# A float32 encoder trunk on one core: q and k products and an output-gate tile placed ahead of the S5 input matrices, the scan shared by two engines, operands moved to PSUM

## The reference, cut to what matters

```python
proj = xn @ w_in                                   # 1024 -> 2048: u, xm, v, o_pre of 512 each
u, xm, v, o_pre = split(proj)
# S5 group: 32 groups of 16 channels, each with 64 complex states
bu = einsum(u, b_bar)                              # b_bar = ((exp(lam*dt) - 1) / lam) * B
states = associative_scan(a_l*a_e, a_l*x_e + x_l)  # diagonal recurrence over the sequence
y = Re(C . states) + D*u ; g = gelu(y) ; y_a = g * sigmoid(g @ w_glu)
# mLSTM group: 4 heads of 128
xc = silu(causal_dwconv(xm, conv_w, conv_b))       # width 4
q, k = xc @ w_q[h], xc @ w_k[h]
gates = concat(q, k, v) @ w_gates + b_gates
h_t = mlstm_chunkwise(q, k, v, gates)              # stabilised matrix memory
y_b = sigmoid(o_pre) * rmsnorm(h_t)
mix = concat(y_a, y_b) @ w_out
```

## Time and profile before

| | |
|---|---|
| median of 3 runs | 1131.56 us (1131.46 to 1132.12) |
| the profiled execution | 1132.59 us, its span 1130.8 us |
| PE busy | 1094.9 us, 97% |
| PEld | 883.0 us, 78% |
| DVE | 649.8 us, 57% |
| ACT | 465.2 us, 41% |
| POOL | 208.8 us, 18% |
| mean granted clock of PE | 0.99 |

### The profile page before, as it was taken

The page is one execution under the profiler, slowest core; times in us unless marked ns, Lnnn a source line. Parts: engine busy times, 40 slices in busy tenths (PEclk is TensorE's granted clock), DMA queues, the critical chain, the costliest instruction groups (busy, mean ns, idle before and its releaser), DMA issues.

```text
span 1130.8 us, 15508 instructions
## 1 busy us (share of the span) xinstructions
PE 1094.9 (97%) x5542; PEld 883.0 (78%) x5542; DVE 649.8 (57%) x871; ACT 465.2 (41%) x671; POOL 208.8 (18%) x312
## 2 busy tenths in 40 slices
...
GB/s 218 167 97 60 91 1 1 167 94 94 93 101 103 93 93 93 96 109 98 107 107 116 68 56 57 21 129 94 106 98 93 93 94 103 99 93 112 94 93 75
DMA packets 36491, 106.73 MB, mean 94 GB/s; under 512 B 7840, under 2 KB 10144, under 8 KB 36320
## 3 DMA queue, kind: packets, MB, share of 16 engines
...
## 4 chain that ended last, share of the span: by engine, by line
PE 82%; DVE 4%; ACT 3%; issue 2%; POOL 0%; DVEq 0%; ACTq 0%; POOLq 0%
PE bank L1401 25%; PE bank L1403 25%; PE bank L1402 25%; PE bank L1743 1%; PE bank L1424 1%; ACT whi L645 1%; PE bank L1765 1%; PE bank L1563 1%; DVE h L1217 1%; PE bank L1596 0%; ACT sq L651 0%; PE bank L1543 0%; DVE xlo L949 0%; DVE wlo L943 0%; POOL ssum L435 0%
## 5 line engine op out<-in xcount | busy, mean ns | idle before, releaser
L1401 PE MATMUL bank<-xhi,whi 128*128 128x512 f32 x992 | 391.4, 395 | 7.6 <-DVE xlo L949 2.9
L1402 PE MATMUL bank<-xlo,whi 128*128 128x512 f32 x992 | 386.7, 390 | 0.0
L1403 PE MATMUL bank<-xhi,wlo 128*128 128x512 f32 x992 | 386.6, 390 | 0.0
L943 DVE TENSOR_TENSOR wlo<-raw,whi 128x1024 fp32r<-128x1024 f32 x177 | 223.5, 1263 | 269.0 <-ACT whi L645 268.4
L645 ACT ACTIVATE whi<-raw 128x1024 fp32r<-128x1024 f32 x177 | 187.1, 1058 | 378.3 <-PE bank L1403 350.6
L1401 PEld LDWEIGHTS bank<-xhi,whi 128*128 128x128 f32 x992 | 186.6, 188 | 52.1 <-issue 6.1
L1403 PEld LDWEIGHTS bank<-xhi,wlo 128*128 128x128 f32 x992 | 186.5, 188 | 39.4
L1402 PEld LDWEIGHTS bank<-xlo,whi 128*128 128x128 f32 x992 | 186.6, 188 | 38.6 <-issue 1.0
L1401 PE MATMUL bank<-ahi,whi 128*128 128x512 f32 (+1 forms) x374 | 142.5, 381 | 0.0
L1403 PE MATMUL bank<-ahi,wlo 128*128 128x512 f32 (+1 forms) x374 | 141.6, 379 | 0.0
L1402 PE MATMUL bank<-alo,whi 128*128 128x512 f32 (+1 forms) x374 | 140.4, 375 | 0.0
...
## 6 DMA issues: line engine op xcount, KB each, us to landing
...
```

The source lines that it names most:

```text
L943: V.tensor_tensor(wlo[:, t % RING, :], raw[:, t % RAWS, :], whi[:, t % RING, :].bitcast(f32), ALU.subtract).then_inc(lo_done, 1)
L1401: MM(dst, wh, rhi, start=start, stop=False)
L1402: MM(dst, wh, rlo, start=False, stop=False)
L1403: return MM(dst, wl, rhi, start=False, stop=stop)
```

## The change

Seven edits, all in the mixer of layer 0:

1. PE: the eight products of q and k, output-gate tile 13 and the gates stand ahead of the S5 transposes and input products. The gates go to bank 7; group b 3 of the transposes waits until DVE has read them.
2. ACT takes q and k out of PSUM, and then rounds tiles 16 and 17, ahead of its copies of the S5 matrices; before, DVE took q out. The S5 matrices lie where the convolution's results did; q and k have places of their own.
3. DVE: the loop makes the remainders up to tile 12; `split_lo(13)` and the three `g_step`s stand behind the loop, then a wait for the gates, their read, and the remainders of tiles 14, 15, 16. `read_out` 0 to 3 come after output gate 0.
4. The clearing of `cdiag` moves to POOL's start, its two copies to ACT ahead of q.
5. The convolution's accumulator is bank 7; in `g_step` one of the two product buffers is bank 5, and the powers are copied to bank 4.
6. The scan: POOL makes four of the seven last sweeps, DVE three, between its last `head_sum` and `head_gate(3)`; PE's S5 output waits for both.
7. ACT loads the table of GELU right behind `head_factor(3)`, and `head_hi(3)` stands ahead of the first GELU.

```diff
@@ layout @@
-O_IN, O_QK, O_O, O_GLU, O_OUT = 0, 12, 16, 20, 24
-O_UP = [32, 102]
+O_IN, O_O, O_GLU, O_OUT = 0, 12, 16, 20
+O_UP = [28, 98]
-IN_BANK = (0, 1, 2, 3, 4, 5, 6, 0, 1, 2, 3, 0, 1, 2, 3, 0, 1, 2, 3, 0)
+IN_BANK = (0, 1, 2, 3, 4, 5, 6, 0, 1, 2, 3, 0, 1, 2, 3, 0)
+QK_BANK = (1, 2, 3, 0)
-    gtmp = at("gtmp", [P, 2, 2, PAIRS, GCH], base)
+    gtmp = at("gtmp", [P, 2, PAIRS, GCH], base)
-    qT = at("qT", [P, HEADS, SEQ], m1_at)
-    kT = at("kT", [P, HEADS, SEQ], m1_at + 8192)
+    m1re = at("m1re", F2, xc_at)
+    m1im = at("m1im", F2, xc_at + 8192)
...
@@ gpsimd @@
+        G.memset(cdiag[:, :, :, :, :], 0.0)
...
+        G.memset(xs[:, 0, :, 0:1], 0.0).then_inc(carry_done, 1)
         a7, b7 = st1[:, :, 0:SUP - 1], st2[:, :, 0:SUP - 1]
-        for i in range(SUP - 1):
+        for i in range(4):
             axpy(XX[:, :, 1:, i], (qk2[:, :, i:i + 1], aj2[:, :, i:i + 1]),
...
@@ scalar @@
-                A(xcf[:, :], cacc[:, :], ACT.Silu).then_inc(xcf_done, 1)
+                A(xcf[:, :], bank[7][:, :], ACT.Silu).then_inc(xcf_done, 1)
...
+        act.wait_ge(c_negated, 1)
+        act.wait_ge(pads_set, 1)
+        for f in range(2):
+            r = slice(STATE * f, STATE * f + STATE)
+            A(cdiag[r, :, :, f, :], bcp[r, 2:4, :].rearrange("p r (j i) -> p r j i", i=GCH),
+              ACT.Copy).then_inc(cdiag_set, 1)
+        for hd in range(HEADS):
+            act.wait_ge(qk_ready, hd + 1)
+            A(qT[:, hd, :], bank[QK_BANK[hd]][:, :], ACT.Copy).then_inc(q_evac, 1)
+        for hd in range(HEADS):
+            act.wait_ge(qk_ready, HEADS + hd + 1)
+            A(kT[:, hd, :], bank[QK_BANK[hd]][:, :], ACT.Copy).then_inc(k_evac, 1)
+        split_hi(T_QK + RING)
+        split_hi(T_O + RING)
         for b in range(8):
             act.wait_ge(m1_ready, b + 1)
...
-        for hd in range(HEADS):
-            act.wait_ge(qk_ready, HEADS + hd + 1)
-            A(kT[:, hd, :], bank[IN_BANK[O_QK + hd]][:, :], ACT.Copy).then_inc(k_evac, 1)
-        split_hi(T_QK + RING)
-        split_hi(T_O + RING)
...
         head_factor(HEADS - 1)
+        act.preload_act_table_set("gelu_apprx_tanh_and_others")
         s5_output(2)
+        head_hi(HEADS - 1)
         s5_gelu(0)
         s5_output(3)
-        head_hi(HEADS - 1)
         s5_gelu(1)
@@ vector @@
+        t5, u5 = gtmp, bank[5][:, :].rearrange("p (r j i) -> p r j i", r=2, i=GCH)
+        qp = bank[4][:, 0:2 * SUP * PAIRS].rearrange("p (r k j) -> p r k j", r=2, j=PAIRS)
         def g_step(s):
-            steps.up(V.tensor_tensor(gtmp[:, 0], gg[:, :, :, 0:GCH], wide(qq[:, 0, s - 1, :]), ALU.mult))
-            steps.up(V.tensor_tensor(gtmp[:, 1], gg[:, :, :, 0:GCH], wide(qq[:, 1, s - 1, :]), ALU.mult))
+            steps.up(V.tensor_tensor(t5[:, :, :, :], gg[:, :, :, 0:GCH], wide(qp[:, 0, s - 1, :]), ALU.mult))
+            steps.up(V.tensor_tensor(u5, gg[:, :, :, 0:GCH], wide(qp[:, 1, s - 1, :]), ALU.mult))
             settle()
             part = slice(s * GCH, (s + 1) * GCH)
-            steps.up(V.tensor_tensor(gg[:, 0, :, part], gtmp[:, 0, 0], gtmp[:, 1, 1], ALU.subtract))
-            V.tensor_tensor(gg[:, 1, :, part], gtmp[:, 0, 1], gtmp[:, 1, 0], ALU.add).then_inc(g_mid, 1)
+            steps.up(V.tensor_tensor(gg[:, 0, :, part], t5[:, 0], u5[:, 1], ALU.subtract))
+            V.tensor_tensor(gg[:, 1, :, part], t5[:, 1], u5[:, 0], ALU.add).then_inc(g_mid, 1)
...
         for t in range(12):
-            if t:
-                wait_tile_used(dve, max(t, 3))
+            wait_tile_used(dve, max(t, 3))
+            if 0 < t < 9:
                 split_lo(t + RING)
-            else:
-                wait_tile_used(dve, 3)
...
-                steps.up(V.tensor_scalar(cacc[:, :], xpad[:, 3:], col("mlw", 4 * m + 3), col("mlb", m),
-                                         ALU.mult, ALU.add))
+                acc = bank[7][:, :]
+                steps.up(V.tensor_scalar(acc, xpad[:, 3:], col("mlw", 4 * m + 3), col("mlb", m), ALU.mult, ALU.add))
...
-                dve.wait_ge(g0_done, 1)
-                dve.wait_ge(q_done, 1)
-            if 8 <= t < 11:
-                g_step(t - 7)
-
-        steps.up(V.memset(cdiag[:, :, :, :, :], 0.0))
...
+        dve.wait_ge(g0_done, 1)
+        dve.wait_ge(q_done, 1)
+        split_lo(T_QK + 1)
+        dve.wait_ge(out_freed, 7)
+        steps.up(V.tensor_copy(qp, qq[:, :, :, :]))
         settle()
-        for f in range(2):
...
-            V.tensor_copy(cdiag[r, :, :, f, :], bcp[r, 2:4, :].rearrange("p r (j i) -> p r j i", i=GCH)
...
+        for step in range(1, 4):
+            g_step(step)
+        dve.wait_ge(gates_ready, 1)
+        V.tensor_scalar(g8[:, :], bank[7][0:104, :], col("bgate", 0, 104), None, ALU.add).then_inc(gates_copied, 1)
+        split_lo(T_QK + 2)
+        split_lo(T_QK + 3)
+        wait_tile_used(dve, T_QK)
+        split_lo(T_QK + RING)
+        out_gate(0)
         for step in range(3):
             read_out(step)
-        dve.wait_ge(m1_ready, 1)
-        for hd in range(HEADS):
-            dve.wait_ge(qk_ready, hd + 1)
-            dve.wait_ge(s5in_ready, 2) if hd == 0 else None
-            V.tensor_copy(qT[:, hd, :], bank[IN_BANK[O_QK + hd]][:, :]).then_inc(out_freed, 1)
         read_out(3)
-        wait_tile_used(dve, T_QK)
-        split_lo(T_QK + RING)
...
-        out_gate(0)
-        dve.wait_ge(gates_ready, 1)
-        V.tensor_scalar(g8[:, :], bank[4][0:104, :], col("bgate", 0, 104), None, ALU.add).then_inc(gates_copied, 1)
...
+        n = SUP - 1
+        a7, b7 = sv1[:, :, 0:n], sv2[:, :, 0:n]
+        for i in range(4, n):
+            dve.wait_ge(carry_done, 1)
+            re, im = qk2[:, :, i:i + 1], aj2[:, :, i:i + 1]
+            steps.up(V.tensor_tensor(a7, re.to_broadcast([P, 2 * PAIRS, n]), XX[:, :, 0:n, SUP - 1], ALU.mult))
+            steps.up(V.tensor_tensor(b7[:, 0:PAIRS], im[:, 0:PAIRS].to_broadcast([P, PAIRS, n]),
+                                     X[1][:, :, 0:n, SUP - 1], ALU.mult))
+            steps.up(V.tensor_tensor(b7[:, PAIRS:], im[:, PAIRS:].to_broadcast([P, PAIRS, n]),
+                                     X[0][:, :, 0:n, SUP - 1], ALU.mult))
+            settle()
+            steps.up(V.tensor_tensor(a7, a7, b7, ALU.add))
+            settle()
+            V.tensor_tensor(XX[:, :, 1:, i], XX[:, :, 1:, i], a7, ALU.add).then_inc(sweep_done, 1)
+            if i < n - 1:
+                dve.wait_ge(sweep_done, i - 3)
         head_gate(HEADS - 1)
@@ tensor @@
+        pe.wait_ge(lo_done, T_QK + 1)
+        pe.wait_ge(xclo_done, HEADS)
+        for b in range(8):
+            hd = b % 4
+            if b < 4:
+                pe.wait_ge(out_freed, max(k + 1 for k in range(12) if IN_BANK[k] == QK_BANK[hd]))
+            else:
+                pe.wait_ge(q_evac, hd + 1)
+            block3(bank[QK_BANK[hd]][:, :], T_QK % RING, b, xchi[:, hd, :], xclo[:, hd, :], True,
+                   True).then_inc(qk_ready, 1)
+        pe.wait_ge(k_evac, 1)
+        project(T_O, O_O)
+        pe.wait_ge(k_evac, HEADS)
+        pe.wait_ge(rms_done, 1)
+        for k in range(12):
+            q = k % 4
+            ins = MM(bank[7][32 * q:32 * q + 8, :], cols("wg")[:, 8 * k:8 * k + 8],
+                     (qT, kT, vT)[k % 3][:, k // 3, :], start=k < 4, stop=k >= 8)
+        ins.then_inc(gates_ready, 1)
         pe.wait_ge(con_in, 16)
         pe.wait_ge(out_freed, 7)
-        pe.wait_ge(rms_done, 1)
         pe.wait_ge(g_built, CH - 4)
         pe.wait_ge(g_mid, 3)
         for b in range(8):
+            if b == 3:
+                pe.wait_ge(gates_copied, 1)
             if b >= 4:
                 pe.wait_ge(m1_copied, b - 3)
...
         pe.wait_ge(scan_done, 1)
+        pe.wait_ge(sweep_done, SUP - 5)
```

More of the change, by code:

```diff
@@ L189, in build @@
     F4 = [P, 2, PAIRS, P]
-    (ff, gg, m1re, m1im, uc, uperm, xchi, xclo, sigo, xs, ksb) = plan(
-        ("ff", F4, f32), ("gg", F4, f32), ("m1re", F2, f32), ("m1im", F2, f32),
+    (ff, gg, qT, kT, uc, uperm, xchi, xclo, sigo, xs, ksb) = plan(
+        ("ff", F4, f32), ("gg", F4, f32), ("qT", [P, HEADS, SEQ], f32), ("kT", [P, HEADS, SEQ], f32),
         ("uc", [P, GROUPS, NCH], f32), ("uperm", [P, 4, SEQ], f32),
@@ L230, in build @@
     pt_at = tail + 4096 + 2112 + 2 * 2048
+    g8 = at("g8", [104, SEQ], pt_at + 4096 + 2560 + 1024 + 64)
     rtmp = at("rtmp", [P, 2, 2, PAIRS, GCH], tail + 4096 + 2112)
@@ L234, in build @@
     st2 = at("st2", [P, 2 * PAIRS, SUP], pt_at + 1024)
+    sv1 = at("sv1", [P, 2 * PAIRS, SUP], pt_at - 4096)
+    sv2 = at("sv2", [P, 2 * PAIRS, SUP], pt_at - 2048)
     fre, fim = ff[:, 0, :, :], ff[:, 1, :, :]
@@ L291, in build @@
     x_back, cdiag_set = sem("x_back"), sem("cdiag_set")
-    g0_done, g_mid, q_done, k_evac, f_done = (sem(n) for n in ("g0_done", "g_mid", "q_done", "k_evac", "f_done"))
+    g0_done, g_mid, q_done, q_evac, k_evac, f_done = (sem(n) for n in (
+        "g0_done", "g_mid", "q_done", "q_evac", "k_evac", "f_done"))
```

(21 more changed lines are left out.)

30 lines of the change are left out of this document (2 added, 28 removed).

## The result

The changed kernel takes 1139.84 us (median of 4, 1139.46 to 1139.98), the kernel before, timed beside it, 1131.84 (1131.46 to 1132.54): a ratio of 1.0069 [1.0052, 1.0087], slower by 8.0 us. The forecast was 1134.8, slower by 3.2. The sign was right, the size was not, and the time lies 0.3 us above the range. Of the 5.0 us between forecast and median, 4.2 are span. The rest is nearly all one correction: the forecast took 1.0 us off because the profiled execution of before lay that far above its median, and the one of after lies only 0.1 above its own.

The account below looks back on a forecast made before the run. PE is busy 97%, so its waits count, the largest 12.6 us ahead of the S5 transposes. First stage +2.3, wait for DVE's sweeps +4.9, GELU reordering -4.0: +3.2 on 1131.56 gives 1134.8 us, range 1129.5 to 1139.5.

Parts of the forecast that it names:

- edit 7's -4.0: S5 output to second transposes: earlier table load and `head_hi(3)` remove the GELU wait and its low clock, -4.0 us.
- The forecast for edit 5: Convolution accumulator in PSUM: speeds DVE by up to 2 us where nobody waits, so value 0, bounds -0.5 and +0.5.
- The first rival: The clock holds through the new gaps: -4.9 us, so 1129.9 and not slower; this side together has chance 0.36.
- The second rival: DVE's and POOL's sweeps overlap and shut each other out: S5 output 4.5 us later, 1139.3; chance 0.10.
- One sign: Among the listed signs of being right: v's transposes start near 113; before 111 would show it wrong.
- There the low stretch went on 3.8 us after PE resumed.: Behind the first gap: clock stays low as long as after the earlier 12.6 us wait, for k's products.
- at half speed 3.5 us do the work of 1.75: k's products after the first gap: low clock adds 1.7 us to their 2.7, ending at 86.5.
- Tile 17's load lands at 101.3.: Second gap: tile 17 rounded by 102.35, first m1 copy at 102.95, so PE idles 6.2 us.
- 1.7 a sweep.: DVE's three scan sweeps ahead of the S5 output: 1.7 us each, 5.1 together.
- sharing saves 6 us: Scan sweeps split between POOL and DVE: S5 output starts at 181.6 instead of 187.9.
- The heads' loop: From v's transposes until PE is ready for the S5 output: everything only shifts, change 0.
- the first stage: From the last projection tile to v's transposes: +2.3 us, bounds -1.5 to +4.5.

Follow-up runs that it names:

- run 4: Kernel before with only the GELU table loaded right behind `head_factor(3)` and `head_hi(3)` ahead of the first GELU: 1128.64 us, ratio 0.9971.
- run 9: Changed kernel with the convolution's accumulator, one `g_step` product buffer and the powers back in SBUF: 1141.85 us, 1.01 against the kernel before.
- run 6: Changed kernel with products nobody reads (24, 31, 9 and 23) in all four TensorE waits: 1135.84 us, 1.0031 against the kernel before.
- run 5: Changed kernel with 24 products nobody reads in the first gap, ahead of k's products: 1139.29 us, 1.007 against the kernel before.
- run 1: Changed kernel with the remainders of tiles 14 and 15 ahead of DVE's wait for the gates: 1132.23 us, 1.0004 against the kernel before.
- run 8: Changed kernel with all seven scan sweeps back on POOL, none on DVE: 1141.55 us, 1.0095 against the kernel before.
- run 10: Changed kernel with tile 17's rounding moved behind ACT's copies of the S5 matrices: 1140.91 us, 1.0082 against the kernel before.
- run 7: Kernel before with 54 products nobody reads in its 12.6 us wait ahead of the S5 transposes: 1133.88 us, ratio 1.0027.
- run 2: Changed kernel with ACT's copies of q and k ahead of tile 15's rounding and of `cdiag`: 1132.07 us, 1.0004 against the kernel before.
- run 3: Changed kernel with q and k copied ahead of tile 15's rounding, and remainders 14 and 15 ahead of the gates' wait: 1126.66 us, 0.9964.

## Why the prediction was right and wrong, by its steps

**Right in kind.** The sequence was as forecast: q's products directly behind the last tile, the wait for q's copy with ACT at tile 15 (5.55 us, forecast 5.6), the second wait for `m1re` behind tiles 16 and 17, the 0.69 and 2.16 us behind it, the clock low in both, the S5 output released by DVE's last sweep, no wait at the GLU, and edit 7's -4.0 (-3.96 in run 4). The forecast for edit 5 is not contradicted (run 9). The first rival, that the clock holds, fell at once; its price of 4.9 us for all the tolls is what run 6 measured, though divided otherwise. The second rival fell too: POOL was done 3.6 us before DVE's first sweep began. One sign was off: v's transposes start at 115.58, not near 113.

**Wrong in size, by 4.2 us of span, at five terms.**

- *"There the low stretch went on 3.8 us after PE resumed."* This is the step that failed first. One stretch of before was used as a fixed toll, and "at half speed 3.5 us do the work of 1.75" came from it. After the first gap it went on for 6.0 us, through all of k's products and into tile 13, and the gates came 1.3 us late (95.94 against 94.6). Run 5 shows that it is the clock: the slow stretch cost 2.8 us there, not 1.7. Part of this is chance: in runs 1, 8 and 10, with the same order and a gap of 5.4 to 5.5 us, the clock was back 4.0 to 5.2 us after TensorE resumed, and the gates ended at 95.65, 95.27 and 95.32. In run 8, the best of them, the stretch cost 1.8 us. So the forecast's 1.7 was the lower edge of what the runs show, and it had no upper one.
- *"Tile 17's load lands at 101.3."* One load of before gave 3.3 us. Two were under way here: tile 16's took 3.3, tile 17's 4.4 (the remainder that frees its place ends at 99.2, the rounding starts at 103.59). In run 6 it was 4.3. That the other load is what slows it was not tested. The second gap was 7.3 instead of 6.2 long, and v's transposes another 0.9 us late. Run 10 shows that this load ended the gap.
- *"1.7 a sweep."* It was 2.15. The durations were scaled from an instruction with contiguous operands, and that one was right (0.39 for `sv<-sv,sv`); those that read or write the scan's strided columns take 0.55, and 0.35 for half of it. Three took 6.4 us instead of 5.1; but the 0.8 us added for contention with POOL did not come, since POOL was done, and DVE came to the sweeps 1.3 us before TensorE was ready, not 1.15, so of the 1.3 only 0.4 reached the wait (5.30, not 4.9). The answer "sharing saves 6 us" went wrong with it, and by POOL's shorter scan (run 8).
- *"It reaches the second transposes at 193.1: -4.0"* was right for edit 7, but the wait for the sweeps stands in front of the first quarter, and the prediction kept before's 4.5 us for it. It took 5.41, +0.9. Its price without a low clock is 2.92 (runs 4, 6 and 7), and before's 4.5 was itself a draw (run 4). Behind the same wait it took 4.5 to 5.5 in the other runs.
- *The heads' loop* was forecast as unchanged. It took 0.7 more; TensorE's waits for `wbuf` in it are 3.2 us with a longest of 1.7, and 2.3 and 1.1 in the trace of before. The late remainders are not the reason: runs 2 and 9 keep them, and their waits are 2.0 like those of runs 1 and 3, yet the stretch isn't shorter there (64.8 and 64.9 us). The cause stays open.

2.1 (the first two terms) + 0.4 + 0.9 + 0.7 make the 4.2. The common fault is that each price was taken at one place of the trace of before. Run 7 shows for the clock's toll in the 12.6 us gap that the kernel before isn't faster without it, since DVE's queue makes the next start. The measured +4.42 for the first stage lies within its bounds (-1.5 to +4.5), as do the sweeps' 5.30 and the -3.05 at the S5 output; what the range did not allow for is that all terms err to the same side together, and the heads' loop had no bounds at all.

## What to carry to other kernels

When a product is moved ahead, walk each in-order queue that its readers and its successors' loads stand in: here three roundings of ACT and two remainders of DVE became 12.8 us of TensorE's idle time, and moving them by a few lines turned +0.7% into -0.4%, a better order into -1.2%. A gap of 5 us or more on the critical engine cost here its length and a slow stretch behind it whose price varied by 2 us, so give it a range, and price the next gap behind it as well. Before counting a saved toll, look for the engine that reaches the next handover just as late.

## What the runs showed of the chip

- The slow stretch behind a gap has no fixed length. It went on for 3.8 us after 12.6 us of waiting, 6.0 after 5.55, and some 5.3 after 5.30. Behind second gaps of 7.1 to 7.3 us in the same order, the S5 products took 2.09 us in two profiled runs (the changed kernel, run 5) and 3.68 or 3.69 in three (runs 2, 8 and 9). In the first two the clock fell some 3.7 us into the gap and was back 3.4 us after TensorE resumed; in the other three it fell some 2.8 us into it and was back only after some 9.1. Why it falls sooner or later was not found.
- Products whose results nobody reads kept the granted clock at 1.00 through waits of 5 to 12 us (runs 5 to 7).
- A DVE instruction on the scan's strided columns costs more than one on `sv` alone: 0.56 us (`xs<-xs,sv`) against 0.39 (`sv<-sv,sv`) for 128x224.
- Of two loads of the weight stream under way together, the second was ready 4.4 us after the remainder that freed its place, the first 3.3.
- The convolution's product with its accumulator in PSUM takes 0.78 us beside a working POOL, with it in SBUF 1.24 (2.34 and 3.73 for three).
